# Eight more tokens leave the dense expert tables: 376 columns a matmul where 384 were, and what moves with them

## What is computed

```python
        s1, i1 = lax.top_k(s[:, :, 0], PEER_TOPK)
        s2, i2 = lax.top_k(s[:, :, 1], PEER_TOPK)
...
        g = jax.nn.softmax(cs, axis=-1)
        ug = jnp.take(u_table, eidx, axis=0)
        vg = jnp.take(v_table, eidx, axis=0)
        hid = jnp.einsum('cd,chkd->chk', xc, ug).astype(jnp.float32)
        a = jax.nn.gelu(hid, approximate=False) * g
        return jnp.einsum('chk,chkd->cd', a.astype(vg.dtype), vg)
```

## Time and profile before

| | |
|---|---|
| median of 3 runs | 2488.97 us (2488.15 to 2490.45) |
| the profiled execution | 2488.55 us |
| its span, first to last instruction | 2486.8 us |
| mean granted clock of TensorE | 0.998 |
| busy: TensorE, VectorE, ScalarE, GpSimd | 2452.5, 1806.6, 1164.4, 514.3 us |

### The profile page before, as it was taken

One profiled execution on the slowest core, in us unless ns is written; L12 is line 12 of the kernel. 1 busy time (PEld: TensorE's weight loads), 2 busy tenths in 40 slices (PEclk: granted clock), 3 DMA queues, 4 the chain that ended last, 5 costly groups with the idle time before them and its releaser, 6 DMA issues.

```text
span 2486.8 us, 35440 instructions
## 1 busy us (share of the span) xinstructions
PE 2452.5 (99%) x13553; PEld 2231.7 (90%) x13553; DVE 1806.6 (73%) x3399; ACT 1164.4 (47%) x1970; POOL 514.3 (21%) x340
## 2 busy tenths in 40 slices
PE   8999999999999999999999999999999999999998
PEld 7788989999999999999999999888788888888887
DVE  7876678999998886798888987878786335533323
ACT  6555465467767776333333335444422223422222
POOL 3222074132222442364444400000000000000000
PEclk9999999999999999999999999999999999999999
DMA  4211344689988999999999972322474332223331
GB/s 170 69 61 43 119 161 165 212 309 322 321 300 296 351 393 346 390 389 389 389 387 390 384 270 76 103 81 84 142 269 152 102 101 95 85 93 102 98 101 39
DMA packets 191240, 519.15 MB, mean 209 GB/s; under 512 B 15896, under 2 KB 67096, under 8 KB 187872
## 3 DMA queue, kind: packets, MB, share of 16 engines
q1 hardware_dynamic: 154208, 382.66, 43.7%
q0 software_dynamic: 36864, 134.23, 14.7%
HBM read 464.34 MB, written 52.49 MB: 208 GB/s over the span
## 4 chain that ended last, share of the span: by engine, by line
PE 90%; DVE 7%; ACT 2%; issue 1%; DMA 0%; DVEq 0%; SPq 0%; ACTq 0%
PE P L1284 28%; PE P L1286 27%; PE P L1285 27%; PE P L1630 2%; DVE wl L1742 1%; PE P L1291 1%; DVE D L1742 1%; DVE T L1745 0%; ACT wh L2396 0%; PE P L1563 0%; PE P L1562 0%; PE P L1561 0%; PE P L1540 0%; PE P L1541 0%; PE P L1539 0%
## 5 line engine op out<-in xcount | busy, mean ns | idle before, releaser
L1284 PE MATMUL P<-XH,wh 128*128 128x512 f32 (+2 forms) x2272 | 839.7, 370 | 6.1 <-DVE wl L1742 6.0
L1286 PE MATMUL P<-XH,wl 128*128 128x512 f32 (+2 forms) x2272 | 823.0, 362 | 0.0
L1285 PE MATMUL P<-XL,wh 128*128 128x512 f32 (+2 forms) x2272 | 822.4, 362 | 0.0
L2396 ACT ACTIVATE wh<-raw 128x1024 fp32r<-128x1024 f32 x458 | 482.6, 1057 | 399.7 <-PE P L1286 397.1
L1742 DVE TENSOR_TENSOR wl<-raw,wh 128x1024 fp32r<-128x1024 f32 x422 | 513.1, 1224 | 92.7 <-ACT wh L2396 92.7
L1284 PEld LDWEIGHTS P<-XH,wh 128*128 128x128 f32 x2272 | 427.5, 188 | 52.2 <-DVE wl L1742 8.8
L1286 PEld LDWEIGHTS P<-XH,wl 128*128 128x128 f32 x2272 | 427.0, 188 | 47.6
L1285 PEld LDWEIGHTS P<-XL,wh 128*128 128x128 f32 x2272 | 428.0, 188 | 42.7 <-issue 1.9
L1284 PE MATMUL P<-AH,wh 128*128 128x384 f32 x1024 | 342.9, 335 | 1.7 <-DVE wl L1742 1.7
L1286 PE MATMUL P<-AH,wl 128*128 128x384 f32 x1024 | 342.1, 334 | 0.0
L1285 PE MATMUL P<-AL,wh 128*128 128x384 f32 x1024 | 342.1, 334 | 0.0
(11 more groups left out here) (326 smaller groups left out, 3259.6 us busy)
## 6 DMA issues: line engine op xcount, KB each, us to landing
raw<-wts SPq DMA_DIRECT2D x211, 512.0 KB, 3.6
raw<-ut SPq DMA_DIRECT2D x128, 512.0 KB, 6.4
raw<-vt SPq DMA_DIRECT2D x128, 512.0 KB, 11.1
hdram<-HID SPq DMA_DIRECT2D x64, 384.0 KB, 4.3
gdram<-GS SPq DMA_DIRECT2D x24, 1024.0 KB, 6.1
GI<-gdram SPq DMA_DIRECT2D x16, 1536.0 KB, 15.0
HI<-hdram SPq DMA_DIRECT2D x32, 768.0 KB, 15.3
AWC<-adat SPq DMA_DIRECT2D x64, 256.0 KB, 5.4
```

The costliest lines, as they stand in the source:

```text
L1284: e.matmul(bank, wh[:, w], H, start=start, stop=False)
L1285: e.matmul(bank, wh[:, w], L, start=False, stop=False)
L1286: return e.matmul(bank, wl[:, w], H, start=False, stop=stop)
L2396: return e.activation(dst, src, ACT.Copy)
```

## The change

The first 8 tokens (NX) leave the dense way as well. Their 8 x 128 experts fill 128 partitions eight times: a partition has one token and half a head (8 of its 128 experts). Matmuls of both tables take columns 8 to 383, that is 376; only unit 0 of the second table keeps 384, with zeros. The gates of those tokens aren't made (two grid steps fewer). Their indices and gates go through HBM into that order (`extra_index`, `extra_load`); their rows of the activations are spread over partitions (XR on VectorE, turned by eight transposes on TensorE, copied to XTX by ScalarE); eight more dots stand among the others from place 44 on. LATE becomes 8, so 128 dots stand beside the first table (116 before) and 144 gathers beside the second (140 before); the pace of dots and axpys is set anew. Beside the second table their sum (SUMX) is added into the PSUM banks by eight products with TOKEN, after unit 64. The gates in HBM are laid out by groups of eight units, so that GI reads one piece of 12 KB a partition and GS is written in pieces of 512 bytes (before, GI was read in pieces of 512 bytes and GS written in 8 KB). At the second table's end, low parts are made ahead of the last operand, unit 127 runs one row behind the three others, and the norm's epsilon of the first norm goes into a gain (gboth) in place of two products with ones_eps for each half.

```diff
-LATE = 12
+LATE = 8
+NX = 8
+PARTS = 128 // NX
+AMONG = 44
+NDOT = 128 - LATE + NX
+NROW = LATE + NX + 128
+STEP0 = NX // 4
+GROUP0 = NX // 16
...
-        for s in range(128 - LATE):
-            if s + 3 < 128 - LATE:
+        for s in range(NDOT):
+            if s + 3 < NDOT:
...
+        yield ("extra_index",)
...
-        for n in range(98):
-            if n in (0, 32):
+        for n in range(STEP0, 98):
+            if n in (STEP0, 32):
                 more, due = route_more(n // 32 + 1), 0.0
             if n in (30, 62):
                 for piece in more:
                     yield piece
                 yield ("gate_turn", n // 32 + 1)
-            if n % 2 and n > 2:
+                if n == 30:
+                    yield ("extra_rows",)
+            if n == STEP0 + 4:
+                yield ("extra_load",)
+            if n % 2 and n > STEP0 + 2:
                 yield ("grid", n - 3)
                 yield ("grid", n - 2)
                 yield 1.5
             if n < 96:
                 yield ("hot", n)
-            if 0 <= n - 1 < 96:
+            if STEP0 <= n - 1 < 96:
                 yield ("weigh", n - 1)
-            yield 1.6 if n % 2 and n > 2 else 3.1
-            due += 3.0 if n < 32 else 4.0
+            yield 1.6 if n % 2 and n > STEP0 + 2 else 3.1
+            due += 3.2 if n < 32 else 4.0
             while due > 0:
                 piece = next(more, None)
                 if piece is None:
...
                 yield piece
                 if not isinstance(piece, tuple):
                     due -= piece
-            dots_due += 1.2 if n < 30 else 1.0 if n < 62 else 1.4
+            dots_due += 1.2 if n < 30 else 1.1 if n < 62 else 1.62
             yield from some(int(dots_due))
             dots_due -= int(dots_due)
-        yield from some(128)
+        yield from some(NDOT)
...
+        yield ("both_gains",)
...
-        for s in range(LATE + 128):
-            if s + 5 < LATE + 128:
+        for s in range(NROW):
+            if s + 5 < NROW:
                 yield ("gather_v", s + 5)
             if s < LATE:
                 yield ("dot_late", s)
+            elif s < LATE + NX:
+                yield ("extra_axpy", s - LATE)
             else:
-                yield ("axpy", s - LATE)
+                yield ("axpy", s - LATE - NX)
             if s == LATE - 1:
                 yield ("dots_end", 1)
-            yield 6.2
+            yield 6.0
...
+        if i == 64:
+            yield ("extra_sum",)
...
             yield ("active_low", 126)
-            yield from activate(127)
-            yield ("active_low", 127)
 
 
     yield from side.rest()
-    for i in range(124, 128):
+    yield from feed.next_unit()
+    yield from feed.low_to(U_V + 128)
+    yield from activate(127)
+    yield ("active_low", 127)
+    for i in range(3):
         yield from feed.next_unit()
+    for i in range(124, 127):
+        yield ("tile", U_V + i, 0)
     for d in range(8):
-        for i in range(124, 128):
-            yield ("tile", U_V + i, d)
+        if d < 7:
+            for i in range(124, 127):
+                yield ("tile", U_V + i, d + 1)
+        yield ("tile", U_V + 127, d)
...
+        for s in (1, 0):
             yield ("square2", s, d)
         if d > 1:
-            for s in range(2):
+            for s in (1, 0):
...
-            yield ("table", 0)
             yield from feed.low_to(U_RET + 3)
     feed.done = U_RET
-    yield ("warm", 9, 0)
+    yield ("warm", 7, 0)
...
-        dg = nc.dram_tensor("gdram", [24, 128, 128, 16], F32, kind="Internal").ap()
+        dg = nc.dram_tensor("gdram", [16, 128, 24, 128], F32, kind="Internal").ap()
...
+        def dot_slot(n):
+            extra = AMONG <= n < AMONG + NX
+            return extra, n - AMONG if extra else n if n < AMONG else n - NX
...
-                    e.dma_start(dg[g], GS[g % 2][:, :, :]).then_inc(d_grid[g % 2], 16)
+                    s.wait_ge(s_gs, n - STEP0 + 1)
+                    if g >= GROUP0 + 2:
+                        s.wait_ge(d_grid[g % 2], 16 * grid_writes(g - 2))
+                    e.dma_start(dg[:, :, g, :].rearrange("j p x -> p j x"), GS[g % 2][:, :, :].rearrange(
+                        "p (j i) t -> p j (i t)", j=16)).then_inc(d_grid[g % 2], 16)
...
+                elif g == 0:
+                    s.wait_ge(s_xturn, 1)
+                else:
+                    s.wait_ge(s_rows, 1 + AMONG + NX)
                 if g % 2 == 0:
-                    s.wait_ge(d_grid[0], 16 * 12)
-                    s.wait_ge(d_grid[1], 16 * 12)
+                    s.wait_ge(d_grid[0], 16 * grid_writes(22))
+                    s.wait_ge(d_grid[1], 16 * grid_writes(23))
                     n = g // 2
-                    e.dma_start(GI[n % 2][:, :, :], dg[:, :, 8 * n:8 * n + 8, :].rearrange(
-                        "g p i t -> p g (i t)")).then_inc(d_gi[n % 2], 16)
+                    e.dma_start(GI[n % 2][:, GROUP0:24, :], dg[n, :, GROUP0:24, :]).then_inc(d_gi[n % 2], 16)
...
-                    H, L = H[:, 0:ND], L[:, 0:ND]
+                    H, L = H[:, NX:ND], L[:, NX:ND]
...
+                    w = slice(NX if i else 0, ND)
                     if i == 0:
                         v_bank(k)
                     p.wait_ge(s_al, i + 1)
-                    t = product(P[k][:, 0:ND], u, k, AH[i % 4][:, :], AL[i % 4][:, :], i == 0, i == 127)
+                    t = product(P[k][:, w], u, k, AH[i % 4][:, w], AL[i % 4][:, w], i == 0, i == 127)
...
+            def extra_rows():
+                p.wait_ge(s_extra, 4)
+                p.wait_ge(s_gtv, 2)
+                p.wait_ge(s_it, 2)
+                p.wait_ge(s_keyc, 16)
+                for k in range(8):
+                    t = e.transpose(P[4 + k // 4][:, 128 * (k % 4):128 * (k % 4) + 128],
+                                    XR[:, k, :, :].rearrange("p t q -> p (t q)"), ident[:, :])
+                t.then_inc(s_xturn, 1)
+
+            def extra_sum():
+                p.wait_ge(s_rows, rows_done(LATE + NX - 1))
+                p.wait_ge(s_const, 2)
+                for d in range(8):
+                    t = e.matmul(P[d][:, 0:NX], SUMX[:, 128 * d:128 * d + 128], TOKEN[:, :], start=False, stop=False)
 
...
-                p.wait_ge(s_sum2[0], 6)
-                e.matmul(P[1 + half][:, w], ones_eps[:, :], TB[0][:, w], start=False, stop=False)
-                p.wait_ge(s_sq2[0], 8)
-                e.matmul(P[1 + half][:, w], ones_eps[:, :], square_slot2(0, 7)[:, w], start=False, stop=False)
...
             def first_ones():
                 p.wait_ge(s_h, 15)
+                p.wait_ge(s_sum2[0], 6)
+                p.wait_ge(s_sq2[0], 8)
...
-                if n == 2:
+                if n == 2 and k == 2:
...
+            def extra_rows():
+                H, L = (part[:, :, 0:NX].bitcast(F32).unsqueeze(3).to_broadcast([128, 8, NX, PARTS])
+                        for part in (XH, XL))
+                tt(XR[:, :, :, :], H, L, ALU.add).then_inc(s_extra, 1)
...
+                extra, k = dot_slot(n)
+                rows_, sums = (XTX, HSX) if extra else (XT, HS)
...
-                    e.activation(dst, hT[:, k, :], ACT.Square, scale=GF[:, k:k + 1]).then_inc(s_sq2[1], 1)
+                    c.wait_ge(s_both, 2)
+                    e.activation(dst, hT[:, k, :], ACT.Square, scale=gboth[:, k:k + 1]).then_inc(s_sq2[1], 1)
```

189 lines of the change are left out of this document (131 added, 58 removed).

## The result

The changed kernel takes 2499.25 us (median of 7 runs, 2496.85 to 2505.13), the kernel before 2489.48 (7 runs): ratio 1.0041, 95% interval 1.0031 to 1.0050. It is slower by 0.4%, where the forecast was 0.4% faster, and it lies outside the range. The profiled execution is the fastest of the seven, 2496.85 us, 8.3 over the 2488.55 of before.

What follows compares the result with a forecast made beforehand. The prediction took TensorE's distance between matmul starts as the bound, with VectorE and DMA nearly full. Its terms summed to -9.7 us from 2488.55, so 2478.9, stated as 2479.0 us; range 2470 to 2488, 8 in 10.

Steps and rivals of the forecast that it cites:

- width, second table: Second table: eight columns fewer save 0.080 us a unit over 127 units, -10.2 us.
- width, first table; two grid steps; extra_index: First table: narrower matmuls in 110 units -8.8 us; two grid steps fewer -0.9; two small VectorE operations +0.5.
- the extra rows' turn: First table, behind the gate transposes: TensorE idles 2.5 us for XR, eight transposes add 0.9; +3.4 us.
- the end of the first table: Leftover background: four grid steps +3.8, later second-table start +1.9, overfull DMA queues +3.3; +9.0 us in all.
- extra_sum: Second table: eight f32 products between two units, 16 passes costing 0.4 to 1.8 us; +1.2 taken.
- the last unit's wait: Second table's end: low parts made ahead shorten TensorE's waits before the last unit, -1.2 us.
- root and last row: Norm after the second table: without ones_eps products and the wait for other sums, -2.7 us (-1.5 to -3.1).
- the price of a column: TensorE matmuls in both tables: 0.417 ns a column plus fixed 13 ns, so 376 columns take 170.0 ns.
- rival 4: Both tables: the narrower matmul doesn't pay; 2498 us, chance 0.03.
- The full queues: Late first table: DMA share 1.11 against at most 1.05, 9 us of work not fitting; a third taken, +3.3 us.
- rival 1: End of first table: the tail is covered, no 3.3 from queues, some 4 of 5.7 remains; 2474 us, chance 0.25.
- Rival 3: First table: dots wait for gathers into four GB buffers; landing in 11 us gives 2493 to 2496, chance 0.07.

Runs made afterwards that it cites:

- the ladder: Changed kernel, 32 units of one table given varied column ranges: first table (where 512 columns ran) 2499.88 us; second table (where the clock stayed at 1.00) 2488.85 us.
- the two ladders: Changed kernel with varied column ranges in 32 units: of the second table, 2488.85 us; of the first, read and written columns set apart, 2499.88 us.
- the table read from 16: Changed kernel with dots spread (2.55 for 2.85 ticks), its first table's 376 columns read from column 16 instead of 8: 2488.81 us, against 2492.10 without this edit.
- the same ladder: First execution of the changed kernel with 32 second-table units given 16 column ranges, at granted clock 0.849: 2671.09 us.

## Why the prediction was wrong, step by step

Where the changed kernel's units start against the kernel before's gives each term in the profiled executions:

| step | predicted | measured |
|---|---|---|
| ahead of the tables | 0 | -0.5 |
| width, second table | -10.2 | 0.0 |
| width, first table; two grid steps; extra_index | -8.8, -0.9, +0.5 | -2.4 together |
| the extra rows' turn | +3.4 | +3.5 |
| the end of the first table | +9.0 | +8.9 |
| extra_sum | +1.2 | +1.8 |
| the last unit's wait | -1.2 | -1.2 |
| root and last row | -2.7 | -1.5 |
| sum | -9.7 | +8.6 |

(The sum is at TensorE's last matmul; the executions' own times differ by 8.3. One pair of grid steps, about 1.0 us, moved from the middle of the first table to its end: at 947 us the kernel before has four pairs to go and the changed one five. It is in the -2.4 as a gain and in the +8.9 as a loss.)

**The step that failed** is the price of a column: "a column costs (173.3 - 120.0)/128 = 0.417 ns on top of a fixed 13 ns, and 376 columns should take 170.0 ns". The fixed part isn't fixed: 376 columns, read from 0 or 8, have one that is 8 cycles longer than that of 384, and 8 columns are 8 cycles, so the saving is taken back. That cost at least 17 of the 19 us, and with it the sign; in the first table, too, a unit without a grid step takes 4.16 us in both kernels. What came is rival 4 (2498), which had 0.03 because "The rows, which give a slope between 256 and 384 columns only, are all for it paying". They said nothing of 376; an untried width should have had a lower bound of no gain. A third width wouldn't have warned. The kernel before has one, and nine distances of 512 columns take 2.04 us, 226.7 ns each, where the line of the other two gives 226.6:

```profile
2199.78 0.39 PE L1285 MATMUL P<-XL,wh 128*128 128x512 f32 x1
...
2201.82 0.39 PE L1285 MATMUL P<-XL,wh 128*128 128x512 f32 x1
```

Three widths that are multiples of 128 lie on a line; between them 320 columns (146.3 ns) lie on it too and 376 don't.

The rule of the Trainium skill that was weighed there ("TensorE: Matmul & The Clock Gate", Back-to-back issue gap: 81 ns at 128 columns, 131 at 512) would have had the width pay a third. No run here shows it: 512 columns take 228 ns in the ladder, and the width paid nothing.

**Right by mechanism and size:** the turn (2.56 idle against 2.5), and the last unit's wait. extra_sum took 0.11 us a product, the upper of its two bounds; I had taken two thirds of it.

**Right in its sum, by luck:** the end of the first table. The four steps took 5.76 us, against the 1.9 of two pairs, +3.9 where 3.8 was said. The second table's start waited 1.48 us, and 0.67 at unit 3. The full queues (+3.3) didn't come: from unit 64 to 116 the changed kernel falls behind nowhere, at a share of 1.05 where 1.11 was reckoned, so rival 1 was right on that. In their place came a price that the working left out: the 15 matmuls behind the idle time ran at 1.2 GHz and took 4.6 us instead of 2.6 (981.17 to 985.82).

**Half right:** the root. The norm follows the last hT after 4.87 us (1540.23 to 1545.10) where it was 7.56, -2.7 as reckoned, but the reordered rows hold that hT back by 1.1.

**The queues.** GI's median landing fell from 15.0 to 9.4 us and the second table's loads from 11.1 to 9.3, while the first table's loads rose from 6.4 to 7.3, where GS's short pieces now are:

```profile
raw<-ut SPq DMA_DIRECT2D x128, 512.0 KB, 7.3
raw<-vt SPq DMA_DIRECT2D x128, 512.0 KB, 9.3
...
GI<-gdram SPq DMA_DIRECT2D x16, 1536.0 KB, 9.4
```

The side of it that the prediction named is right: the queue with the short pieces gives way. It cost nothing: a load of the first table was issued 18.4 us (median) ahead of ScalarE's use of it, and TensorE's only wait between 500 and 970 us is the one for XR. Rival 3 (gathers) didn't come: GB took 7.8 us to land, and VectorE's idle time for it is 9.7 us over the whole table.

**Shown and only argued.** That the width pays nothing, and that the order at the end costs 7 us, is shown by undoing each alone. That the part on top of the columns hangs on the count and the first column read is shown by the two ladders and by the table read from 16. That the clock falls behind the waits of 2.5 to 2.9 us in some of the profiled executions and not in others is shown; what decides it isn't. Why these counts and columns, and not others, stays open: no row shows what TensorE waits for between two starts.

## What to carry to other kernels

Measure the pace of the very shape and first column that an edit will use before a sum rests on it: one execution with a few odd units tells, and known widths on either side don't. When a width can be chosen, choose by that table; here 16 tokens out won 31 us over 8, for the same code. And look at what a background still owes when its cover ends: what is poured out there costs its own wait, in some executions the matmuls' clock behind it, and with that a steady time.

## What the runs showed of the hardware that was not expected

- The distance of matmul starts isn't a line in the columns, though 256 (120.0 ns), 384 (173.3) and 512 (226.7) lie on one in the kernel before: 376 columns take 173.1 ns and 372 166.8 to 170.0, 352 take 160.8 read from column 0 and 166.7 from 32, and 256 116.8 from 8 and 119.4 from 128. The column that is written doesn't matter.
- At a granted clock of 0.85 the same ladder was a plain proportion (0.490 ns a column, no fixed part), so the pattern found at 1.00 didn't hold there (one execution).
- The same idle time can cost the clock or not. Behind 2.74 us without work the granted clock was 0.50 in the changed kernel's execution, with matmuls 0.31 us apart up to 985.6; behind 2.73 us at the same place in the ladder's it stayed at 1.00.
